# One-hot rows of a PEER layer: from 128-column operations on two engines to eight tokens per operation on VectorE

## What is computed

```python
eidx = jnp.take_along_axis(cidx, ti, axis=-1)      # i * 128 + j
g = jax.nn.softmax(tv, axis=-1)
a = jnp.einsum('cd,ced->ce', xb, utab[ib]).astype(jnp.float32)
coef = (gb * jax.nn.gelu(a, approximate=False)).astype(xb.dtype)
return jnp.einsum('ce,ced->cd', coef, vtab[ib])
```

## Time and profile before

| | |
|---|---|
| median of the runs | 4055.96 us |
| the profiled execution, and its span | 4056.58 us, 4054.8 us |
| TensorE busy | 3708.7 us (91%) |
| VectorE busy | 2613.5 us (64%) |
| ScalarE busy | 1290.4 us (32%) |
| GpSimd busy | 1191.9 us (29%) |
| mean granted TensorE clock | 0.956 |
| `stage_gates` | 2146 to 2916 us |

### The profile page before, as it was taken

The page is one execution under the profiler, slowest core; times in us unless marked ns, Lnnn a source line. Parts: engine busy times, 40 slices in busy tenths (PEclk is TensorE's granted clock), DMA queues, the critical chain, the costliest instruction groups (busy, mean ns, idle before and its releaser), DMA issues. The chain is left out here.

```text
span 4054.8 us, 54674 instructions
## 1 busy us (share of the span) xinstructions
PE 3708.7 (91%) x19170; PEld 3237.6 (80%) x19170; DVE 2613.5 (64%) x5657; ACT 1290.4 (32%) x2513; POOL 1191.9 (29%) x797
## 2 busy tenths in 40 slices
PE   6879899998887979899999999999779999999997
PEld 3579888887666768799998988989668888888875
DVE  5563033221555421599998888889767777777777
ACT  1110122221114221223326777777622222222220
POOL 1132112211331111123334444434243333333340
PEclk9789899998999989999999999999989999999998
DMA  4751212113554222333337999999987787888882
GB/s 171 286 184 34 88 58 75 71 72 139 203 182 168 81 88 78 104 129 126 133 119 247 320 337 321 339 316 336 299 312 286 287 291 290 292 292 294 288 306 110
DMA packets 502565, 826.52 MB, mean 204 GB/s; under 512 B 289031, under 2 KB 309767, under 8 KB 496296
## 3 DMA queue, kind: packets, MB, share of 16 engines
q1 hardware_dynamic: 111704, 370.02, 25.7%
q0 software_dynamic: 84096, 318.80, 21.4%
q10 hardware_dynamic: 306576, 135.28, 13.3%
HBM read 679.30 MB, written 144.70 MB: 203 GB/s over the span
## 5 line engine op out<-in xcount | busy, mean ns | idle before, releaser
L79 PE MATMUL va_fps<-va_vt_h,va_c_h 128*128 128x512 f32 x1536 | 606.5, 395 | 62.8 <-DVE va_vt_l L2209 27.4
L80 PE MATMUL va_fps<-va_vt_l,va_c_h 128*128 128x512 f32 x1536 | 604.1, 393 | 0.0
L81 PE MATMUL va_fps<-va_vt_h,va_c_l 128*128 128x512 f32 x1536 | 603.6, 393 | 0.0
L2087 POOL DMA_INDIRECT va_rows<-in_vtab,k_pick x256 | 392.1, 1532 | 648.6 <-DVE k_big L2233 573.4
L79 PE MATMUL ga_aps<-k_u_h,k_ut_h 128*128 128x384 f32 x1152 | 403.1, 350 | 10.7 <-DVE k_ut_l L1989 7.0
L1914 ACT ACTIVATE ga_first<-ga_first,ga_gs 128x128 f16<-128x128 f16 x1152 | 357.8, 390 | 162.4 <-DVE ga_first L1973 161.9
L79 PEld LDWEIGHTS va_fps<-va_vt_h,va_c_h 128*128 128x128 f32 x1536 | 292.5, 190 | 127.7 <-issue 35.4
L81 PE MATMUL ga_aps<-k_u_h,k_ut_l 128*128 128x384 f32 x1152 | 391.1, 340 | 0.0
L80 PE MATMUL ga_aps<-k_u_l,k_ut_h 128*128 128x384 f32 x1152 | 390.4, 339 | 0.0
L2233 DVE SCALAR_TENSOR_TENSOR k_big<-va_rows,va_coef,k_big 128x1024 f32<-128x1024 f32 x254 | 321.1, 1280 | 62.8 <-DMA va_rows<-in_vtab,k_pick 60.7
L80 PEld LDWEIGHTS va_fps<-va_vt_l,va_c_h 128*128 128x128 f32 x1536 | 292.7, 191 | 60.8
(11 more groups left out here) (296 smaller groups left out, 8064.5 us busy)
## 6 DMA issues: line engine op xcount, KB each, us to landing
k_ut<-in_utab SPq DMA_DIRECT2D x129, 512.0 KB, 3.5
va_vt<-in_vtab SPq DMA_DIRECT2D x128, 512.0 KB, 6.9
va_c<-scratch_ahead SPq DMA_DIRECT2D x128, 384.0 KB, 3.4
va_wt<-scratch_gates SPq DMA_DIRECT2D x128, 384.0 KB, 5.1
hy_tab<-in_tab POOLq DMA_DIRECT2D x64, 512.0 KB, 4.8
scratch_ahead<-ga_gelu_a ACTq DMA_DIRECT2D x72, 384.0 KB, 6.5
sp_wada<-in_w_ada SPq DMA_DIRECT2D x24, 1024.0 KB, 8.4
scratch_gates<-ga_wide ACTq DMA_DIRECT2D x32, 768.0 KB, 14.6
```

Source lines behind the costliest of these rows:

```text
L79: nc.tensor.matmul(out, w[0], x[0], start=first, stop=False)
L80: nc.tensor.matmul(out, w[0], x[1], start=False, stop=False)
L81: return nc.tensor.matmul(out, w[1], x[0], start=False, stop=last)
L2087: nc.gpsimd.indirect_dma_start(got[:, q % SLOTS_G, :], None, vrows, picked(K, q)).then_inc(got_in[q % SLOTS_G], 16)
```

## The change

The numbers 0 to 127 and the picks' indices are kept in half precision. Each index and each of the share's two parts is stored twice, side by side, and the one-hot tiles are seen as 64 pairs of columns: with that, one operation of two tensors runs over eight tokens at once (`BATCH`), its innermost two columns contiguous in every operand and the broadcast one dimension further out. The double indices lie in a part of `u_l` that the dense products don't read.

- `stage_select`: ScalarE copies the indices of 128 tokens twice into half precision, and the share in a second operation; GpSimd converts the row of numbers to half precision once, at its end.
- `stage_gates`, VectorE: `hits(m)` makes `first` and `second` of eight tokens (two operations), `weigh(m)` multiplies `first` by the share's low and high part (two operations). Between the two stand the dots. At the stage's start VectorE scales the shares and stores both parts twice.
- ScalarE weighs nothing any more.
- Three sets of one-hot tiles of eight tokens (before: four of four). `hits(m)` waits until TensorE has used batch m − 3. VectorE is two batches ahead (`LEAD`): it makes batches 0, 1 and 2 in tile 0. From there on, tiles have one, one and two batches in turn.
- TensorE's matmuls are the same in number and order; they read columns of the batch's tiles.

```diff
+BATCH = 8
...
+def pairs_at(K):
+    spare = K["u_l"][:, 0:2 * DENSE // (2 * P), 0:2 * P].bitcast(F16)
+    return spare.rearrange("p (a c) (t b) -> p a c t b", a=2, b=2)
...
             low(0, AT * KT)
+            pool.wait_ge(small, 16)
+            nc.gpsimd.tensor_copy(K["iota16"][:, :], K["iota"][:, :])
...
-                    nc.scalar.activation(K["sel"][:, :, bass.ds((n - GATHERED) * P, P)],
-                                         tps[:, :].rearrange("p (a t) -> p a t", t=P), ACT.Copy).then_inc(t_ok, 1)
+                    into = pairs_at(K)[:, :, bass.ds(i - EARLY, 1), s * P:(s + 1) * P, :].rearrange("p a c t b -> p (a c) t b")
+                    nc.scalar.activation(into, tps[:, 0:2 * P].rearrange("p (a t) -> p a t", t=P).unsqueeze(3)
+                                         .to_broadcast([P, 2, P, 2]), ACT.Copy)
+                    nc.scalar.activation(K["sel"][:, bass.ds((n - GATHERED) * P, P)], tps[:, 2 * P:3 * P], ACT.Copy).then_inc(t_ok, 1)
...
-        first = sb("first", [P, 4, 2, G, NK], F16)
-        second = sb("second", [P, 4, G, NK], F16)
+        SETS = 3
+        share16 = sb("share16", [P, 2, DENSE, 2], F16)
+        first = sb("first", [P, SETS, 2, BATCH, NK // 2, 2], F16)
+        second = sb("second", [P, SETS, BATCH, NK // 2, 2], F16)
...
+        LEAD = 2
+
+        def batches_of(q):
+            return range(LEAD * (q > 0) + BATCHES * q // TILES, min(BATCHES, LEAD + BATCHES * (q + 1) // TILES))
...
         def rows_after(b):
-            return range(ROWS * b // GROUPS, ROWS * (b + 1) // GROUPS)
+            return range(ROWS * b // BATCHES, ROWS * (b + 1) // BATCHES)
...
+                    for m in (todo[:-1], todo[-1:])[h]:
+                        pe.wait_ge(f_ok, m * G // BATCH + 1)
+                        pe.wait_ge(act_out, m + 1)
...
-            def weigh(m):
-                act.wait_ge(hot_ok, m + 1)
-                b = m % 4
-                for part in (1, 0):
-                    for t in BY_ACT:
-                        at = m * G + t
-                        last = nc.scalar.activation(first[:, b, part, t, :], first[:, b, 0, t, :], ACT.Copy,
-                                                    scale=gs[:, part, at:at + 1])
-                last.then_inc(f_ok, 1)
...
+            shape = [P, BATCH, NK // 2, 2]
+            numbers = K["iota16"][:, :].rearrange("p (a b) -> p a b", b=2).unsqueeze(1).to_broadcast(shape)
+
+            def of_batch(t):
+                return t.unsqueeze(2).to_broadcast(shape)
+
+            def indices(part, m):
+                chunk, at = m * BATCH // (2 * P), m * BATCH % (2 * P)
+                return of_batch(pairs_at(K)[:, part, chunk, at:at + BATCH, :])
+
+            def shares(part, m):
+                return of_batch(share16[:, part, m * BATCH:(m + 1) * BATCH, :])
+
+            def hits(m):
+                if m >= SETS:
+                    dve.wait_ge(mm, 4 + BATCH // G * (m - SETS + 1))
+                b = m % SETS
+                v.tensor_tensor(first[:, b, 0], numbers, indices(0, m), ALU.is_equal).then_inc(hot_ok, 1)
+                v.tensor_tensor(second[:, b], numbers, indices(1, m), ALU.is_equal)
+
+            def weigh(m):
+                dve.wait_ge(hot_ok, m + 1)
+                b = m % SETS
+                for part in (1, 0):
+                    last = v.tensor_tensor(first[:, b, part], first[:, b, 0], shares(part, m), ALU.mult)
+                last.then_inc(f_ok, 1)
+
+            scaled, pairs = K["sel"], [P, DENSE, 2]
+            hits(0)
+            ch.link(v.tensor_scalar(scaled[:, :], scaled[:, :], GATE_SCALE, None, ALU.mult))
+            ch.link(v.tensor_copy(share16[:, 0], scaled[:, :].unsqueeze(2).to_broadcast(pairs)))
+            ch.link(v.tensor_tensor(share16[:, 1], scaled[:, :].unsqueeze(2).to_broadcast(pairs), share16[:, 0], ALU.subtract))
+            weigh(0)
...
-            for i in range(TURNS):
-                for q in range(TILES):
-                    for b in groups_of(q):
-                        one_hot(GROUPS * i + b, b % 4)
-                        for j in rows_after(b):
-                            dot(i, j)
-                    low(1 - q % 2, TILES * i + q + 1)
+            for n in range(TILES):
+                for m in batches_of(n):
+                    if m:
+                        hits(m)
+                    for j in rows_after(m):
+                        dot(j)
+                    if m:
+                        weigh(m)
+                low(1 - n % 2, n + 1)
```

More of the change, by code:

```diff
@@ L1793, in stage_gates @@
         TW = 48
-        iota = sb("iota", [P, NK], F16)
-        gh16 = sb("gh16", [P, DENSE], F16)
-        gs = sb("gs", [P, 2, DENSE])
-        first = sb("first", [P, 4, 2, G, NK], F16)
-        second = sb("second", [P, 4, G, NK], F16)
+        SETS = 3
+        share16 = sb("share16", [P, 2, DENSE, 2], F16)
+        first = sb("first", [P, SETS, 2, BATCH, NK // 2, 2], F16)
+        second = sb("second", [P, SETS, BATCH, NK // 2, 2], F16)
         flat = K["big"][:, :, :].rearrange("p a b -> p (a b)")
@@ L1809, in stage_gates @@
         chain_s, f_ok, mm, act_out = (sem(n) for n in ("chain", "f_ok", "mm", "act_out"))
-        shares_ok, hot_ok = sem("shares_ok"), sem("hot_ok")
+        hot_ok = sem("hot_ok")
         ut_hi, ut_ok, a_mm, gelu_ok, dot_ok = (sem(n) for n in ("ut_hi", "ut_ok", "a_mm", "gelu_ok", "dot_ok"))
@@ L1816, in stage_gates @@
         block = ctx.enter_context(nc.Block())
[L1817 to L1821, removed]
+        TILES = BESIDE
+        GROUPS = DENSE // G
+        BATCHES = DENSE // BATCH
+        ROWS = GATHERED * PICKS
         BLOCK = TW // G
@@ L1828, in groups_of, with columns @@
             return range(GROUPS * q // TILES, GROUPS * (q + 1) // TILES)
+        LEAD = 2
+        def batches_of(q):
+            return range(LEAD * (q > 0) + BATCHES * q // TILES, min(BATCHES, LEAD + BATCHES * (q + 1) // TILES))
+        def columns(t):
+            return t.rearrange("p a b -> p (a b)")
         def rows_after(b):
-            return range(ROWS * b // GROUPS, ROWS * (b + 1) // GROUPS)
+            return range(ROWS * b // BATCHES, ROWS * (b + 1) // BATCHES)
         @block.sync
@@ new lines, in _ @@
+            for n in range(TILES):
+                s, todo = n % 2, list(groups_of(n))
+                pe.wait_ge(ut_ok, n + 3)
+                for h in range(2):
+                    pe.wait_ge(gelu_ok, 2 * n + h + 1)
+                    cut = dense_half(h)
+                    for k in range(KT):
+                        last = product3(nc, aps[:, 2 * s + h, 0:DH], (ut_h[:, s, k, :], ut_l[:, s, k, :]),
+                                        (u_h[:, k, cut], u_l[:, k, cut]), k == 0, k == KT - 1)
+                    last.then_inc(a_mm, 1)
+                    for m in (todo[:-1], todo[-1:])[h]:
+                        pe.wait_ge(f_ok, m * G // BATCH + 1)
+                        pe.wait_ge(act_out, m + 1)
+                        b = m * G // BATCH % SETS
+                        for t in range(G):
+                            for part in range(2):
+                                last = nc.tensor.matmul(ps[:, m % 4, t * NK:(t + 1) * NK], columns(second[:, b, m * G % BATCH + t, :, :]),
+                                                        columns(first[:, b, part, m * G % BATCH + t, :, :]), start=part == 0, stop=part == 1)
+                        last.then_inc(mm, 1)
@@ L1906, in store @@
                               wide[block % 2][:, lo:hi, :]).then_inc(done, 16)
-            def weigh(m):
-                act.wait_ge(hot_ok, m + 1)
-                b = m % 4
-                for part in (1, 0):
-                    for t in BY_ACT:
-                        at = m * G + t
-                        last = nc.scalar.activation(first[:, b, part, t, :], first[:, b, 0, t, :], ACT.Copy,
-                                                    scale=gs[:, part, at:at + 1])
-                last.then_inc(f_ok, 1)
[L1918 to L1921, removed]
             waiting = []
             for n in range(BESIDE):
-                i, q, a = n // TILES, n % TILES, n % 2
+                a = n % 2
                 split(1 - a, n + 1, n // 2)
                 act.wait_ge(act_stored[a], 16 * (n // 2 + 1))
-                todo = list(groups_of(q))
+                todo = list(groups_of(n))
                 for h in range(2):
                     gelu(a, n, h)
[L1930 to L1933, removed]
+                    for m in (todo[:-1], todo[-1:])[h]:
                         if m % BLOCK == 0 and m // BLOCK >= 2:
@@ L1958, in _ @@
             dve.sem_inc(ut_ok, 3)
[L1959 to L1978, removed]
@@ L1980, in dot @@
-            def dot(i, j):
-                k, turn = j % SLOTS_G, ROWS // SLOTS_G * i + j // SLOTS_G
+            shape = [P, BATCH, NK // 2, 2]
[5 more added lines that the diff above has]
+                return of_batch(pairs_at(K)[:, part, chunk, at:at + BATCH, :])
@@ L1982, in dot @@
```

(11 more changed lines are left out.)

## The result

4089.98 us, the median of four runs (4084.34 to 4093.45), against 4055.09 before, there too the median of four: ratio 1.0084, with a 95% interval of 1.0067 to 1.0102. The change makes the kernel 35 us, 0.8%, slower, inside the forecast range and 5 us above the forecast. The profiled execution took 4093.45 us.

The account below looks back on a forecast made before the run. The changed stage was taken as bound by TensorE's work, 62 us of waits and clock. Terms −61.8 − 13 + 64 + 23 + 16 gave +28 to +29 us on 4056.58: forecast 4085, range 4040 to 4130.

Parts of the forecast that it names:

- Relief: Changed stage: TensorE's waits for ScalarE's weighings and for `low` go, −61.8 us, and the clock lost behind them, −13 us.
- 0.61 a step: VectorE's new half-precision operations of 1024 columns take 0.61 us a step, 2.44 us for eight tokens.
- rival 3: The stored pairs are not packed: VectorE's operations take 1.15 us a step, +130 us, 4185; chance 0.06.
- The queue in front of `low`: VectorE's in-order batches delay `low`: TensorE waits 1.91 us per three tiles, 2.8 with gathers, +64 us over 23 periods.
- Clock: TensorE's matmuls run slow behind the new waits on `low`, 1.5 us lost each, +23 us.
- Start: Tile 0: VectorE makes three batches before `low(1)`, so TensorE idles 13.6 us, plus 2.6 of slow clock: +16 us.
- Sum: All terms together: +28 to +29 us on the profiled execution of 4056.58, forecast 4085.
- Rival 2: Even: D's chain as walked, landings in time, clock lost once in three: −3 us, 4053; chance 0.12.
- D's chain: VectorE's fourth batch in three tiles waits for TensorE's mid-tile group, so `low` comes late, mean 1.91 us.
- Rival 4: DMA queues hold the stage: 4110, counted as the forecast with a larger gather term, together 0.62.
- Rival 1: The relief wins, with D's mean wait at 1.2 us and no clock loss: −33 us, 4024; chance 0.2.
- The rule of the Trainium skill: Two-input VectorE operations make every GpSimd gather refill 0.75 us later, growing the gather term by up to 15 us.

Follow-up runs that it names:

- e3: Changed kernel with every index and share read as one element with an innermost step of zero instead of the stored pair: 4198.22 us, ratio 1.0344.
- e4: Changed kernel without the stage's gathers but for the first four: 4050.94 us, ratio 0.9978 to before.
- e11: Changed kernel with the gates stored in runs of 2880 bytes in place of 192: 4086.35 us, ratio 1.0080 to before.
- e6: Changed kernel with a lead of one batch instead of two and ScalarE's split moved ahead of its two DMA issues: 4045.72 us, ratio 0.9979.
- e10: e6 with the gates of all but the last token block stored in runs of 2880 bytes in place of 192: 3998.42 us, ratio 0.9849.
- e7: Kernel before the change with only ScalarE's split moved ahead of its DMA issues: 4049.58 us, ratio 0.9987.
- e9: e6 without the stage's gathers but for the first four: 3992.72 us, ratio 0.9838.

## Why the prediction was right

- *Relief, −61.8 and −13.* Shown for the largest part: waits for weighed groups fell from 53.4 us to under 1. The other parts, 8.4 us for `low` and the clock, can't be told apart from what came in their place.
- *0.61 a step.* Shown: 0.685 long, step 0.60 to 0.61; e3 gives 1.222 for rival 3, and 4198 where 4185 was forecast for it.
- *The queue in front of `low`, 1.91 a period.* 1.80 in e4. With gathers 2.86 (79.0 less the start's 13.2, over 23), forecast 2.8. That this fits so well is partly luck: 0.4 of the 2.8 was an allowance for scattered landings, not worked out, and of the 2.86 about 0.25 goes with large packets (e11 has 2.61), where the walk by median landings had 2.4.
- *Clock, +23.* Granted 0.96 over 805 us is a loss of 32 us, 0.98 over 770 one of 15: 17 more, where −13, +23 and the start's 2.6 made 13. The rows round the clock to two digits, some 4 us either way; what the waits leave of the stage's 35 us is 17 too.
- *Start, +16.* 13.0 us of wait, and behind it a half tile of 6.3 us where 4.26 is usual (2176.28 to 2182.57), so 15; the first dot came 5.7 us later than before, with the stage's start 5.1 us later; the fifth dot stood 7.0 us behind it where 8.9 was walked, `low(1)` 15.5 where 16.8 was.
- *Sum.* +28 forecast, +35 of stage measured, +35 of median: waits +18 (79.0 + 0.8 − 53.4 − 8.4; forecast +16), clock +17 (forecast +13). VectorE also stood 16.6 us for `split`, behind ScalarE's blocked issues, which the prediction did not have.
- *Rival 2, even, 4053.* It supposed landings in time, and e4 without gathers is that case: 4050.94. D's chain as walked thus costs about what the relief saves, and the waits for gathers on top of it make the kernel slower. (The kernel before was not run without its gathers.)
- *Rival 4.* Counted as a larger gather term, it was a mechanism of its own: blocked issues on ScalarE. It had little part in the kernel after (e11) and held e6 (e10), the other mended orders probably too. *Rival 1* priced a relief that wins at 4024; with the order mended e6 ended at 4046.
- *The rule of the Trainium skill* ("SBUF — State Buffer", Who interferes with whom) that a VectorE operation with two SBUF inputs shuts out a GpSimd instruction that reads SBUF. GpSimd's issues were busy 317 us before (172.5 + 144.9) and 338 after (172.8 + 164.9): 0.08 us a refill more, the direction of the rule, but a tenth of the 0.75 us that I made of it. In e3, where the same two-input operations take 1.222 us, the issues were busy 452 us, 0.45 a refill more than in the kernel after.

## What to carry to other kernels

A quicker operation shortens the whole only where another engine waits for what its engine does next. On an engine that works in order, walk its queue, and put the short operation that releases the bottleneck ahead of any that waits for the bottleneck's later progress. Three buffers with a lead of two leave one batch that waits in the middle of a tile; a lead of one did not need it. When several orders end at the same length, look for a shared resource, and test it by taking away packets and bytes one at a time. When the experiments turn up a repair that has nothing to do with the change, give it to the old kernel too before comparing (e7).

## What was not expected of the hardware

- A DMA issue on ScalarE's queue took up to 12.8 us (median 4.4, e6) with stores in 192-byte packets beside gathers; never more than 0.36 with the same bytes in 2880-byte runs (e10), nor more than 0.35 with the small packets and no gathers (e4, e9). The profile books it as a wait for nothing ahead of ScalarE's next operation.
- The stage moved 348 GB/s with large packets (e10, DMA share 0.95) and 324 with small ones (e6, share 1.10), the same bytes from the same program.
- Reading one stored half-precision value with an innermost step of zero takes 1.222 us for 1024 columns, reading it as a stored pair 0.685.
